# Cross-attention with operands split into high and low parts: one kernel before and after

## The reference, cut to what matters

```
def mem_cross_attention(q, mem_n, w_kv):        # mem_n = rms_norm(mem, mem_norm_g[i])
    k, v = split_cols(mem_n @ w_kv, (XA_WIDTH, XA_WIDTH))
    sc = jnp.einsum('bqhd,bkhd->bhqk', q * (XA_HEAD_DIM ** -0.5), k)
    p = jax.nn.softmax(sc, axis=-1)
    return jnp.einsum('bhqk,bkhd->bqhd', p, v)
```

## Time and profile before

| what | value |
|---|---|
| median of three runs | 1400.44 us |
| lowest and highest | 1399.53, 1400.68 us |
| span of the profiled execution, first to last instruction | 1399.1 us |
| time of the profiled execution itself | not listed apart; the runs stand 0.4 to 1.6 us above its span |
| TensorE busy | 1384.9 us, 99% of the span |
| DVE busy | 924.8 us, 66% |
| ACT busy | 881.0 us, 63% |
| POOL busy | 351.3 us, 25% |
| mean busy share of the DMA engines | mostly 5 to 6 tenths |

### The profile page before, as it was taken

How to read it: one execution, slowest core, us unless ns; L and a number is a source line. 1 busy time by engine, 2 the same in 40 slices (tenths; PEclk the granted TensorE clock), 3 DMA queues, 4 the chain that set the end, 5 groups by cost and what they waited for, 6 DMA issues and landing times.

```text
span 1399.1 us, 22109 instructions
## 1 busy us (share of the span) xinstructions
PE 1384.9 (99%) x8179; PEld 1217.9 (87%) x8179; DVE 924.8 (66%) x1344; ACT 881.0 (63%) x1411; POOL 351.3 (25%) x177
## 2 busy tenths in 40 slices
PE   8999999999999999999999999999999999999998
PEld 8899898888888889888899998988888888888886
DVE  5568575898988455554554775768989874555533
ACT  6566677986755456555446765779776564565543
POOL 1310010111023444444414000112010244444442
PEclk9999999999999999999999999999999999999999
DMA  8665445668655556666655555555666655565663
GB/s 271 199 175 172 130 137 163 168 197 214 197 191 182 182 177 184 194 188 218 196 182 171 168 152 149 145 170 165 201 199 204 199 173 189 169 194 182 194 196 120
DMA packets 158182, 253.85 MB, mean 181 GB/s; under 512 B 12681, under 2 KB 59899, under 8 KB 157819
## 3 DMA queue, kind: packets, MB, share of 16 engines
q1 hardware_dynamic: 157347, 250.73, 58.7%
q10 hardware_dynamic: 728, 1.71, 0.3%
HBM read 250.18 MB, written 2.23 MB: 180 GB/s over the span
## 4 chain that ended last, share of the span: by engine, by line
PE 94%; ACT 3%; DVE 1%; DMA 1%; issue 0%; DVEq 0%; ACTq 0%; SPq 0%
PE PS L676 76%; PE S L676 15%; PE S L683 1%; ACT wH L1032 1%; ACT scr L1189 1%; DVE wL L1418 1%; PE S L938 1%; PE S L1002 0%; PE S L909 0%; DMA w_raw<-in_w_mem_kv_dram 0%; ACT actLf L1063 0%; PE S L881 0%; DMA regA<-in_mem_dram 0%; ACT L1189 0%; ACT L1209 0%
## 5 line engine op out<-in xcount | busy, mean ns | idle before, releaser
L1032 ACT CAST wH<-w_raw 128x1024 fp32r<-128x1024 f32 x436 | 456.1, 1049 | 445.4 <-PE PS L676 302.9
L1418 DVE TENSOR_TENSOR wL<-w_raw,wH 128x1024 fp32r<-128x1024 f32 x326 | 416.3, 1283 | 316.1 <-ACT wH L1032 297.8
L1348 POOL TENSOR_TENSOR wL<-w_raw,wH 128x1024 fp32r<-128x1024 f32 x110 | 269.1, 2447 | 404.2 <-ACT wH L1032 404.2
L676 PE MATMUL PS<-hHL,wH 128*128 128x256 f32 (+1 forms) x2016 | 313.3, 303 | 1.0 <-ACT regA L1051 1.0
L676 PEld LDWEIGHTS PS<-hHL,wH 128*128 128x128 f32 x2016 | 266.2, 190 | 12.0 <-issue 2.6
L676 PE MATMUL PS<-wH,actH 128*128 128x512 f32 x560 | 222.5, 397 | 0.0
L676 PE MATMUL PS<-wH,actL 128*128 128x512 f32 x560 | 218.4, 390 | 0.0
L676 PE MATMUL PS<-wH,hHL 128*128 128x512 f32 x768 | 200.9, 403 | 0.0
L676 PEld LDWEIGHTS PS<-wH,hHL 128*128 128x128 f32 x768 | 139.9, 188 | 33.1 <-issue 6.5
L676 PE MATMUL PS<-hHL,wL 128*128 128x256 f32 x1152 | 167.6, 283 | 0.0
L676 PEld LDWEIGHTS PS<-hHL,wL 128*128 128x128 f32 x1152 | 156.2, 191 | 6.3
(11 more groups left out here) (256 smaller groups left out, 1551.9 us busy)
## 6 DMA issues: line engine op xcount, KB each, us to landing
w_raw<-in_w_in_dram SPq DMA_DIRECT2D x192, 512.0 KB
w_raw<-in_w_ffn_in_dram SPq DMA_DIRECT2D x176, 256.0 KB
w_raw<-in_w_branch_dram SPq DMA_DIRECT2D x64, 512.0 KB
w_raw<-in_w_ffn_out_dram SPq DMA_DIRECT2D x44, 512.0 KB
w_raw<-in_w_mem_kv_dram SPq DMA_DIRECT2D x32, 512.0 KB
regA<-cs_rows SPq DMA_DIRECT2D x64, 256.0 KB, 4.9
w_raw<-in_w_out_dram SPq DMA_DIRECT2D x16, 512.0 KB
regA<-in_mem_dram SPq DMA_DIRECT2D x4, 256.0 KB, 5.7
```

Source lines behind the costliest of these rows:

```text
L676: return nc.tensor.matmul(o, l, r, start=first, stop=last, skip_group_check=True)
L1032: nc.scalar.copy(wH[:, slot], raw[:, slot]).then_inc(h_done[slot], 1)
L1348: nc.gpsimd.tensor_tensor(wL[:, slot], raw[:, slot], wH[:, slot].bitcast(F32), ALU.subtract).then_inc(l_done[slot], 1)
L1418: v.tensor_tensor(wL[:, slot], raw[:, slot], wH[:, slot].bitcast(F32), ALU.subtract).then_inc(l_done[slot], 1)
```

## The change

The cross-attention's products become sums of three single-pass products, like the large ones: keys, values, queries and probabilities are each kept as a high part in fp32r and a low part. The high part is written by ACT and the low part by DVE, which then frees the PSUM tile. For mk, mv and xq alike both happen at the position after the group's last unit (4, 8, 12, 16, 26 and 34). The keys are no longer scaled; instead the scores are multiplied by `mrow` in the same operation that takes their maximum, which writes the scaled scores to SBUF, and the exponentials read them there. The copy of the transposed probabilities becomes a copy on ACT and a new step of DVE, `xa_split`, at the same position. The tiles move: keys and queries lie in the areas of the activations' high and low parts, the values in two other areas, and several names are second views of the same memory.

```diff
--- before.py
+++ after.py
@@ -118,9 +118,9 @@
     late = {("q", 0): 1, ("z", 0): 2, ("k", 1): 1, ("z", 2): 1, ("v", 0): 2, ("xbc", 1): 1, ("z", 3): 2}
     put(6, "dve", "mem_row")
     for g, (kind, b, units, _) in enumerate(GROUPS):
-        if kind == "mk":
-            put(FIRST_UNIT[g] + units + (2 if b == 0 else 1), "dve", "mk", g)
-        if kind in ("mv", "xq", "q", "k", "v", "xbc", "z", "gate0", "gate1", "gate2"):
+        if kind in ("mk", "mv", "xq"):
+            put(FIRST_UNIT[g] + units, "dve", "split_low", g)
+        if kind in ("mk", "mv", "xq", "q", "k", "v", "xbc", "z", "gate0", "gate1", "gate2"):
             put(FIRST_UNIT[g] + units + late.get((kind, b), 0), "act", "evac", g)
 
     for i in range(7):
@@ -169,6 +169,7 @@
         put(u + 3, "dve", "xa_norm", h)
         put(u + 4, "pe", "xa_turn", h)
         put(u + 5, "act", "xa_copy", h)
+        put(u + 5, "dve", "xa_split", h)
         put(u + 6, "pe", "xa_values", h)
         put(u + 7, "act", "xa_high", h)
         put(u + 7, "dve", "xa_low", h)
...
@@ -345,7 +354,10 @@
 
         DA_A, SSM_A, XA_A, MEM_A, MRG_A = 0, 8, 24, 24, 0
 
-        mkT, mvN, xqT = v3(actHf[:, T * (SSM_A + 8):T * (SSM_A + 16)], KT), v3(regA[:, 2048:4096], NT), v3(regA[:, 4096:6144], KT)
+        mkH, mkL = actH[:, SSM_A + 8:SSM_A + 16, :], actL[:, SSM_A + 8:SSM_A + 16, :]
+        xqH, xqL = actH[:, DA_A:DA_A + 8, :], actL[:, DA_A:DA_A + 8, :]
+        mvH = [v3(regAr[:, 2048 + 1024 * i:3072 + 1024 * i], NT) for i in range(2)]
+        mvL = [v3(regBr[:, 3072 + 1024 * i:4096 + 1024 * i], NT) for i in range(2)]
         BT, CT = v3(regA[:, 0:1024], SG), v3(regA[:, 1024:2048], SG)
         xsN = [v3(actHf[:, T * (SSM_A + 4 * g):T * (SSM_A + 4 * g + 4)], NT) for g in range(SG)]
         gain_rows = v3(regB[0:8, 3072:3328], DEPTH)
...
@@ -869,9 +883,11 @@
                         wait_evacuated(pe, lay, "mk", 1)
                     take(lay, i % 2)
                     for t in range(NT):
-                        for k in range(2):
-                            ins = mm(S[i % 2][:, T * t:T * (t + 1)], xqT[:, 2 * i + k, P * t:P * (t + 1)],
-                                     mkT[:, 2 * i + k, :], k == 0, k == 1)
+                        o, q = S[i % 2][:, T * t:T * (t + 1)], slice(P * t, P * (t + 1))
+                        for k in (2 * i, 2 * i + 1):
+                            mm(o, xqH[:, k, q], mkH[:, k, :], k == 2 * i, False)
+                            mm(o, xqL[:, k, q], mkH[:, k, :], False, False)
+                            ins = mm(o, xqH[:, k, q], mkL[:, k, :], False, k == 2 * i + 1)
                     ins.then_inc(xa_sc, 1)
                 elif kind == "xa_turn":
                     take(lay, 2)
@@ -885,9 +901,11 @@
                     take(lay, 3)
                     pe.wait_ge(xa_copied, XH * lay + i + 1)
                     for e in range(2):
+                        o, q = S[3][:, T * e:T * (e + 1)], slice(T * (i % 2) + P * e, T * (i % 2) + P * (e + 1))
                         for k in range(2):
-                            ins = mm(S[3][:, T * e:T * (e + 1)],
-                                     mvN[:, k, T * i + P * e:T * i + P * (e + 1)], attT[:, k, :], k == 0, k == 1)
+                            mm(o, mvH[i // 2][:, k, q], attH[:, k, :], k == 0, False)
+                            mm(o, mvL[i // 2][:, k, q], attH[:, k, :], False, False)
+                            ins = mm(o, mvH[i // 2][:, k, q], attL[:, k, :], False, k == 1)
                     ins.then_inc(xa_pv, 1)
                 elif kind == "da_scores":
                     half, j = i // HALF, i % HALF
@@ -1035,12 +1053,13 @@
                 kind, b = GROUPS[g][:2]
                 pair = g % 2
                 src = PS[pair]
-                if kind in ("xq", "q", "k"):
+                if kind in ("mk", "xq"):
                     wait_full(act, lay, g)
-                    if kind == "xq" and lay == 0 and b == 0:
-                        act.wait_ge(mem_stored, 16)
-                    dst = xqT[:, 4 * b:4 * b + 4, :] if kind == "xq" else (qT if kind == "q" else kT)[b]
-                    nc.scalar.copy(dst, v3(src[:, :], 4)).then_inc(psum_free[pair], 1)
+                    dst, done = (mkH, mem_kv_h) if kind == "mk" else (xqH, xq_h)
+                    nc.scalar.copy(dst[:, 4 * b:4 * b + 4, :], v3(src[:, :], 4)).then_inc(done, 1)
+                elif kind in ("q", "k"):
+                    wait_full(act, lay, g)
+                    nc.scalar.copy((qT if kind == "q" else kT)[b], v3(src[:, :], 4)).then_inc(psum_free[pair], 1)
                 elif kind == "v":
                     wait_full(act, lay, g)
                     nc.scalar.copy(vN[b], v3(src[:, :], NT)).then_inc(psum_free[pair], 1)
@@ -1048,9 +1067,9 @@
                     act.wait_ge(mem_diag, lay + 1)
                     wait_full(act, lay, g)
                     for t in range(NT):
-                        ins = nc.scalar.activation(mvN[:, t, UC * b:UC * (b + 1)], src[:, UC * t:UC * (t + 1)], ACT.Copy,
+                        ins = nc.scalar.activation(mvH[b][:, t, :], src[:, UC * t:UC * (t + 1)], ACT.Copy,
                                                    scale=mr[:, t:t + 1])
-                    ins.then_inc(psum_free[pair], 1)
+                    ins.then_inc(mem_kv_h, 1)
                 elif kind == "xbc":
                     wait_full(act, lay, g)
                     n = CONV_ORDER.index(b)
@@ -1170,15 +1189,12 @@
                     b = i % 2
                     act.wait_ge(xa_max, XH * lay + i + 1)
                     for t in range(NT):
-                        ins = nc.scalar.activation(sc[b][:, T * t:T * (t + 1)], S[b][:, T * t:T * (t + 1)], ACT.Exp,
-                                                   bias=nmx[b][:, t:t + 1], scale=1.0 / 16.0,
-                                                   accum_out=sm[b][:, t:t + 1])
-                    ins.then_inc(side_free[b], 1)
+                        nc.scalar.activation(sc[b][:, T * t:T * (t + 1)], sc[b][:, T * t:T * (t + 1)], ACT.Exp,
+                                             bias=nmx[b][:, t:t + 1], scale=1.0 / 16.0, accum_out=sm[b][:, t:t + 1])
                     act.drain().then_inc(xa_exp, 1)
                 elif kind == "xa_copy":
                     act.wait_ge(xa_turned, XH * lay + i + 1)
-                    nc.scalar.copy(attT, v3(S[2][:, :], 2)).then_inc(side_free[2], 1)
-                    act.drain().then_inc(xa_copied, 1)
+                    nc.scalar.copy(attH, v3(S[2][:, :], 2)).then_inc(xa_att_h, 1)
                 elif kind == "xa_high":
                     act.wait_ge(xa_pv, XH * lay + i + 1)
                     nc.scalar.copy(actH[:, XA_A + 2 * i:XA_A + 2 * i + 2, :], v3(S[3][:, :], 2)).then_inc(xa_h, 1)
@@ -1645,17 +1661,36 @@
                     dve.wait_ge(mem_bcast, lay + 1)
                     v.tensor_copy(mrow, S[0][:, 0:T]).then_inc(side_free[0], 1)
                     dve.drain()
-                elif kind == "mk":
-                    b = GROUPS[i][1]
-                    wait_full(dve, lay, i)
-                    v.tensor_tensor(mkT[:, 4 * b:4 * b + 4, :], v3(PS[i % 2][:, :], 4),
-                                    mrow.unsqueeze(1).broadcast_to([P, 4, T]), ALU.mult).then_inc(psum_free[i % 2], 1)
+                elif kind == "split_low":
+                    name, b = GROUPS[i][:2]
+                    src = PS[i % 2]
+                    if name == "xq":
+                        dve.wait_ge(xq_h, 2 * lay + b + 1)
+                        q = slice(4 * b, 4 * b + 4)
+                        low(xqL[:, q, :], v3(src[:, :], 4), xqH[:, q, :]).then_inc(psum_free[i % 2], 1)
+                    elif name == "mk":
+                        dve.wait_ge(mem_kv_h, 4 * lay + b + 1)
+                        q = slice(4 * b, 4 * b + 4)
+                        low(mkL[:, q, :], v3(src[:, :], 4), mkH[:, q, :]).then_inc(psum_free[i % 2], 1)
+                    else:
+                        dve.wait_ge(mem_kv_h, 4 * lay + 2 + b + 1)
+                        for t in range(NT):
+                            ins = low(mvL[b][:, t, :], src[:, UC * t:UC * (t + 1)], mvH[b][:, t, :], mr[:, t:t + 1])
+                        ins.then_inc(psum_free[i % 2], 1)
                 elif kind == "xa_max":
                     b = i % 2
                     dve.wait_ge(xa_sc, XH * lay + i + 1)
-                    v.tensor_reduce(mx[b][:, 0:2], v3(S[b][:, :], 2), AX.X, ALU.max)
+                    for t in range(NT):
+                        q = slice(T * t, T * (t + 1))
+                        ins = v.tensor_tensor_reduce(sc[b][:, q], mrow, S[b][:, q], 1.0, -3.0e38, ALU.mult, ALU.max,
+                                                     mx[b][:, t:t + 1])
+                    ins.then_inc(side_free[b], 1)
                     dve.drain()
                     v.tensor_scalar(nmx[b][:, 0:2], mx[b][:, 0:2], -1.0 / 16.0, None, ALU.mult).then_inc(xa_max, 1)
+                elif kind == "xa_split":
```

(17 more changed lines are left out.)

## The result

The changed kernel takes 1419.41 us (median of 4 runs, 1417.35 to 1422.01) against 1400.56 us for the kernel before in the same comparison: a ratio of 1.0132, 95% interval 1.012 to 1.0144. It is 18.9 us slower. The forecast was 1413.1 with a range of 1408.0 to 1418.0: the direction was right, the size was not. The profiled execution took 1419.29 us, with a span of 1417.5, which is 18.4 more than before.

The account below looks back on a forecast made before the run. TensorE's summed work was taken to bound the kernel: -4.5 products, +11.4 xq1, +2.8 mv1, +1.1 position 4, +1.9 clock gave +12.7 us, so 1400.44 becomes 1413.1 us, range 1408.0 to 1418.0.

Parts of the forecast that it names:

- What bounds the kernel: Whole kernel: time is the sum of TensorE's work, and any wait put in front of it is lost in full.
- The products: Cross-attention scores and values: 16 products at 1.44 us instead of 1.72 us each, saving 4.5 us.
- The hand-back of xq1: Scores of head 0 wait for DVE's subtraction at position 34: 5.7 us per layer, 11.4 us in two.
- The hand-back of mv1: Unit 18 waits for DVE's two subtractions behind ACT's scaling copies: 1.4 us per layer, 2.8 us in both.
- position 4: Layer 0 alone: DVE's mk0 step stands before the norm factors' reciprocal, adding 1.1 us to TensorE's wait.
- What stays hidden: Other added ACT copies, DVE subtractions and `xa_split` in the cross-attention: finished before they are needed, costing nothing.
- TensorE's clock: Behind the two waits for xq1: one fall to the lower clock level taken, 1.9 us, out of 0, 1.9 or 3.8.
- DVE as the bound of the whole part: Rival: added subtractions pile up, weights' low parts come late and TensorE waits in many places; 1422 us, chance 6%.
- DVE in time at position 34: Rival: the wait at xq1 is 0.7 instead of 5.7 us and no clock falls; 1401.2 us, chance 5%.
- everything hidden: Third rival: the hand-back through two engines is hidden everywhere and the products alone decide; 1395.9 us, chance 3%.

Follow-up runs that it names:

- late_wait: Changed kernel with the wait for xq1 before the scores of head 2 instead of head 0; 1402.56 us, ratio 1.001.
- token: Kernel before plus one empty DVE step at position 34, for which the scores of head 0 wait; 1415.59 us, ratio 1.0106.
- mk0_back: Changed kernel with DVE's low part of mk0 moved back from position 4 to position 6; 1416.73 us.
- before_mv1: Kernel before with one move, ACT evacuating mv1 at position 15, ahead of the cast of unit 19; 1399.09 us, ratio 0.9986.
- warm40: Changed kernel with 40 matmuls of constants run on TensorE in front of the wait for xq1; 1415.58 us.
- warm20: Changed kernel with 20 matmuls of constants run on TensorE in front of the wait for xq1; 1416.10 us.
- all3: Changed kernel with xq1's wait at head 2, mk0's low part at position 6, mv1's evacuation one position earlier; 1398.03 us, ratio 0.9979.
- all4: all3 with ACT signalling each half of mv on its own, so DVE starts earlier; 1397.20 us, ratio 0.9973.
- all5: all4 with DVE making the norm factors' diagonals at position 3 instead of 4; 1394.39 us, ratio 0.9963.

## Why the prediction was right and wrong

**What bounds the kernel**: right. TensorE's waits were lost in full; no later wait took any of them up.

**The products**: right, -4.5 us. The new matmuls are 0.12 us apart (135.93, 136.05), 12 of them take 1.44 us, from 135.93 to 137.37. The figure of 109 ns from the Trainium skill (TensorE: Matmul & The Clock Gate, Back-to-back issue gap) would have given 6.6; the trace does not agree with it for pairs of load and matmul.

**The hand-back of xq1**: right in place, cause and size. 5.71 us in layer 0 against 5.7. In layer 1 it was 6.05: DVE there paused for 0.43 us before an operation, in a stretch in which any pause of DVE is passed on. late_wait and token show the mechanism from both sides.

**The hand-back of mv1** (1.44 us against 1.4) and **position 4** (1.2 against 1.1): right as waits. What the clock did behind them is the step below.

**What stays hidden**: right but for one wait of the attention that grew by 0.4 us in all. Why it grew was not tested.

**TensorE's clock**: this is the step that failed, a term that was mis-sized. I wrote "I take one fall, 1.9 us" and the profile has three, 6.5 us in all. Two mistakes lie in it. The first: only the two waits for xq1 were asked about. The wait behind unit 5 was priced at its 1.1 us alone, although it grew from 2.10 to 3.36 us, and for the row of 2.10 I had inferred from one execution that such a wait does no harm. mk0_back and before_mv1 have the same wait at 2.24 and 2.31 us with a low clock behind it: the one profile of before had shown one outcome of two. The same holds for the waits at unit 18: grown from 0.49 to 1.93 us, they were priced without a fall too. In the changed kernel's profile that came true, but three other traces with the same wait (mk0_back, warm40, warm20) lost 1.5 us each there, so part of it is luck of the execution. The second: between two rows far apart I took the middle for waits of over 5 us, which were near the bad end; both lost the clock. The sentence on the Trainium skill (TensorE: Matmul & The Clock Gate, HAM oscillation) had both falling, 1415.0 us; the trace agrees with it on both gaps, and 1415.0 is still 4.4 us short, 2.4 of it the third fall. The cost of one fall was well judged: 1.9 against 2.4, 2.3 and 1.8; over all traces it lies between 1.5 and 2.6.

The range ended at 1418.0, since it allowed two falls and some more waiting. Three falls and the measured waits come to 1400.44 + 18.3 = 1418.7, and the median was 1419.41. With two falls, as the range allowed, the same sum would have been 1416.3.

**The rivals.** DVE as the bound of the whole part did not come true: no low part of weights stands among TensorE's waits. DVE in time at position 34, and everything hidden, fell with the first profile. all3 shows what the third would have needed: not a faster DVE, but a wait that asks for what head 0 reads.

## What to carry to other kernels

Before an evacuation gets a second engine, look at what that engine does at that place in its own order, not at its mean load: DVE was idle for a third of the whole run, and 5 us late at the one spot that counted. Then ask whether the waiting engine waits for data that it reads or for a count that happened to be free before. And where an engine with a clock of two levels is kept waiting, price each wait that appears or grows at the wait and up to one fall of the clock, as long as several executions, and not one, have not shown otherwise. Here every wait of over 4 us at the scores lost the clock, and the waits at unit 18, of 1.9 us, lost it in some executions.

## What the runs showed of the hardware that was not expected

- TensorE's clock can fall after waits of about 2 us, and not in every execution. The traces of all kernels, one execution each, by the length of TensorE's idle time at three waits:

| wait | idle before, us | traces | clock fell behind |
|---|---|---|---|
| unit 18, both layers | 0.42 to 0.99 | before, token, all3, all4, all5 | 0 of 10 |
| unit 18, both layers | 1.93 to 1.94 | after, late_wait, mk0_back, warm40, warm20 | 3 of 10 |
| norm factors | 1.75 to 2.10 | token, all3, before | 0 of 3 |
| norm factors | 2.24 to 2.31 | mk0_back, before_mv1, all4 | 3 of 3 |
| norm factors, xq1 | 3.14 to 3.50 | late_wait, warm40, after, warm20 (three) | 5 of 6 |
| xq1, token | 4.65 to 5.90 | token, after, mk0_back | 6 of 6 |

  Each of these 17 falls cost 1.5 to 2.6 us, counted as the distance between starts beyond that of the same matmuls at the high level.
- The time of a run goes with its mean granted clock. Of the 21 runs of the kernel before in one session, the four with a mean granted clock of 0.997 or 0.998 took 1401.84 to 1404.51 us, the 17 others 1400.26 to 1401.75. Only profiled runs have a trace, so where in those four the clock fell is not shown; the wait behind the norm factors is one candidate.
- The clock can fall after the idle time is over: in warm20, layer 1, the matmuls behind the wait ran 0.12 us apart for the last 0.6 us before they became 0.21 apart (820.70 to 821.30, then 821.52). late_wait, warm40 and all4 show the same behind the norm factors.
- At the start of the run the profile of the kernel before gives a granted clock of 1.00 (4.50 to 8.90 us) while matmuls of 256 columns start 0.21 to 0.22 us apart; behind later waits the granted clock and the distances agree. So for the start the distance between starts is the better witness.
